# Half-token stages at the end of a two-block transformer kernel, DVE's share of the weight split, and rounded sums for three norms

## The reference

```
h = h + 0.5 * swiglu(rms(h, ffn1_norm), ffn1_w_in, ffn1_w_out)    # U_F1I, U_F1O
h = h + hybrid_mixer(rms(h, mix_norm), ...)                       # linear attention, sparse attention
h = h + 0.5 * swiglu(rms(h, ffn2_norm), ffn2_w_in, ffn2_w_out)    # U_F2I, U_F2O
h = h + sigmoid(rms(h, ple_norm) @ ple_w_gate) * (p @ ple_w_proj) # U_PLEG; U_PLEP makes the product with p
return rms(h, final_norm)

def rms(x, g):  return x * rsqrt(mean(x * x) + eps) * g
def swiglu(x, w_in, w_out):  gate, up = split(x @ w_in); return (silu(gate) * up) @ w_out
```

## Time and profile before

| | |
|---|---|
| median of 3 runs | 2160.92 us |
| profiled execution | 2160.85 us, its span 2159.0 us |
| PE busy | 2145.0 us (99% of the span) |
| DVE, ACT, POOL busy | 985.5, 756.4, 977.7 us |
| granted TensorE clock, mean of the span | 0.998 of full speed |
| chain that ended last | PE 89%, DVE 4%, POOL 2%, issue 2%, ACT 1% |
| stores of the result | 8 issues on SP, 256 KB each, landing 2.8 us after issue (median) |

### The profile page before, as it was taken

How to read it: one execution, slowest core, us unless ns; L and a number is a source line. 1 busy time by engine, 2 the same in 40 slices (tenths; PEclk the granted TensorE clock), 3 DMA queues, 4 the chain that set the end, 5 groups by cost and what they waited for, 6 DMA issues and landing times.

```text
span 2159.0 us, 31378 instructions
## 1 busy us (share of the span) xinstructions
PE 2145.0 (99%) x12524; PEld 1849.6 (86%) x12524; DVE 985.5 (46%) x1471; ACT 756.4 (35%) x1020; POOL 977.7 (45%) x777
## 2 busy tenths in 40 slices
PE   9999999999999999999999999999999999999998
PEld 8897999999999887888888788888788888888886
DVE  5244454289888208322200719651975442222026
ACT  4133455342222216322212415551346332222134
POOL 3322223466555548555544541054422555555444
PEclk9999999999999999999999999999999999999999
DMA  4321111212222223222222321123220222222222
GB/s 166 103 79 60 60 60 59 98 67 92 96 97 97 107 97 111 104 97 97 97 97 97 103 101 62 40 79 137 78 79 21 98 98 97 97 97 97 97 103 92
DMA packets 31950, 195.18 MB, mean 90 GB/s; under 512 B 3968, under 2 KB 4480, under 8 KB 10096
## 3 DMA queue, kind: packets, MB, share of 16 engines
q1 hardware_dynamic: 26784, 182.86, 23.6%
q10 hardware_dynamic: 5072, 11.00, 1.6%
HBM read 189.48 MB, written 4.23 MB: 90 GB/s over the span
## 4 chain that ended last, share of the span: by engine, by line
PE 89%; DVE 4%; POOL 2%; issue 2%; ACT 1%; DMA 0%; SPq 0%; DVEq 0%; ACTq 0%; POOLq 0%
PE ps L2456 75%; POOL wlo L726 2%; PE ps L3104 2%; PE ps L2523 2%; DVE sqa L1578 1%; PE ps L3319 1%; PE ps L3303 1%; PE ps L3239 1%; PE ps L3186 1%; DVE x2lo L1566 1%; PE ps L2771 1%; PE ps L2698 0%; DMA raw<-wstream 0%; PE ps L2733 0%; PE ps L2794 0%
## 5 line engine op out<-in xcount | busy, mean ns | idle before, releaser
L726 POOL TENSOR_TENSOR wlo<-raw,whi 128x512 fp32r<-128x512 f32 (+2 forms) x768 | 973.9, 1301 | 1146.1 <-ACT whi L802 1093.8
L802 ACT CAST whi<-raw 128x2048 fp32r<-128x2048 f32 x161 | 307.7, 1911 | 814.7 <-PE ps L2456 758.4
L2456 PE MATMUL ps<-x2hi,whi 128*128 128x512 f32 x1136 | 449.0, 395 | 1.1 <-DVE x2lo L1566 1.1
L2456 PE MATMUL ps<-x2hi,wlo 128*128 128x512 f32 x1136 | 442.4, 389 | 0.0
L2456 PE MATMUL ps<-x2lo,whi 128*128 128x512 f32 x1136 | 442.1, 389 | 0.0
L2456 PE MATMUL ps<-xhi,whi 128*128 128x256 f32 (+2 forms) x1304 | 263.2, 283 | 0.9 <-DVE xlo L1566 0.5
L2456 PE MATMUL ps<-xlo,whi 128*128 128x256 f32 (+2 forms) x1304 | 260.8, 281 | 0.0
L2456 PE MATMUL ps<-xhi,wlo 128*128 128x256 f32 (+2 forms) x1304 | 260.7, 281 | 0.0
L2456 PEld LDWEIGHTS ps<-x2hi,whi 128*128 128x128 f32 x1136 | 213.3, 188 | 49.0 <-issue 5.0
L2456 PEld LDWEIGHTS ps<-x2lo,whi 128*128 128x128 f32 x1136 | 213.4, 188 | 44.7 <-issue 1.9
L2456 PEld LDWEIGHTS ps<-x2hi,wlo 128*128 128x128 f32 x1136 | 213.2, 188 | 44.8
(11 more groups left out here) (497 smaller groups left out, 2802.4 us busy)
## 6 DMA issues: line engine op xcount, KB each, us to landing
raw<-wstream SPq DMA_DIRECT2D x170, 1024.0 KB, 4.8
ncb<-c_rows ACTq DMA_DIRECT2D x8, 256.0 KB, 3.7
ple_rows<-ple_out ACTq DMA_DIRECT2D x4, 512.0 KB, 3.9
bias<-bias_rows ACTq DMA_DIRECT2D x8, 256.0 KB, 4.7
ple<-ple_rows ACTq DMA_DIRECT2D x4, 512.0 KB, 5.3
out_dram<-outb SPq DMA_DIRECT2D x8, 256.0 KB, 2.8
h_all<-h SPq DMA_DIRECT2D x1, 792.0 KB, 10.4
h_all<-h SPq DMA_DIRECT2D x2, 264.0 KB, 7.0
```

Of the source, the lines that this page charges most:

```text
L726: return nc.gpsimd.tensor_tensor(wlo[b][:, cols], raw[b][:, cols], whi[b][:, cols].bitcast(F32), ALU.subtract)
L802: nc.scalar.copy(whi[b][:], raw[b][:]).then_inc(sig("hi_done"), 1)
L2456: ins = mm(dst, w[slot][:, cols], xx(tok), start=first and p_ == 0, stop=last and p_ == 2, skip_group_check=True)
```

## The change

It has four parts.

1. *The start of U_F1I.* POOL makes only three quarters of the low weights of the first two units. DVE makes the other five inside `add_normed`, one after each of chunks 4 to 7 and one at the end. TensorE's order takes k = 0 and 1 of both units first. U_F1I+2 is rounded by quarters.
2. *Norms 4, 6 and 7* (both feed-forwards of the second block, and PLE). ACT copies the sum of squares rounded to fp32r, DVE subtracts this from the sum, and TensorE multiplies both parts by fp32r ones. The sum moves 12 matmuls later, into the unit that follows (for norm 7 behind 24 instead of 12 matmuls of U_PLEG+1). For all folded norms the refinement writes `fold` itself, without the copy.
3. *The heads' sums* come together behind the whole of U_MG1+1.
4. *The end* goes by halves of the tokens. U_PLEG+2 is scaled by two instructions. The last unit does both chunks for tokens 0 to 255, then chunk 0 and chunk 1 for tokens 256 to 511, each in its own place in PSUM. Sums, root and scaling follow for each half; the root is one power on POOL instead of ACT's and DVE's steps. Blocks 0 and 1 are scaled and stored first.

The diff, cut to its core:

```
-        PIECE = {u: P for u in (U_UP, U_UP + 1, U_PLEP, U_F1I, U_F1I + 1, U_GR + 2, U_GR + 3, U_MG1, U_DSAO + 1)}
+        PIECE = {u: P for u in (U_UP, U_UP + 1, U_PLEP, U_GR + 2, U_GR + 3, U_MG1, U_DSAO + 1)}
+        FIRST_LOW = [(U_F1I, 0), (U_F1I, 1), (U_F1I + 1, 0)]
+        LATER_LOW = {4: (U_F1I, 2), 5: (U_F1I, 3), 6: (U_F1I + 1, 1), 7: (U_F1I + 1, 2), 8: (U_F1I + 1, 3)}
...
+            for part in range(2):                                       # POOL
+                pool.wait_ge(sig("mean_out"), part + 1)
+                cols = slice(2 * part, 2 * part + 2)
+                nc.gpsimd.tensor_tensor(out_root[:, cols], out_mean[:, cols], half_col.to_broadcast([P, 2]), ALU.pow
+                                        ).then_inc(sig("root_out"), 1)
...
+            def sum_high(n):                                            # ACT
+                act.wait_ge(sig("sq_added"), adds_before(n + 1))
+                nc.scalar.copy(sum_split[:, 0, :], squares_of(n)[:, 0, :]).then_inc(sig("norm_half"), 1)
...
+                if n in SPLIT:                                          # DVE, end of folded_sums
+                    dve.wait_ge(sig("norm_half"), 2 * SPLIT.index(n) + 3)
+                    vec.tensor_tensor(sum_split[:, 1, :], squared[:, 0, :], sum_split[:, 0, :].bitcast(F32),
+                                      ALU.subtract).then_inc(sig("norm_half"), 1)
...
+                if n in SPLIT:                                          # TensorE, norm
+                    for x in range(2):
+                        ins = mm(total, one_r.to_broadcast([P, P]), sum_split[:, x, :], start=(x == 0), stop=(x == 1))
...
-                norm()
                 units_of_pair(1, False)
...
-            after_ple = [(0, 0), (0, 1), (0, 2), (1, 0), (1, 1), (0, 3), (0, 4), (1, 2), (0, 5), (1, 3), (0, 6), (0, 7)]
-            after_ple += [(1, k) for k in range(4, KC)]
+            after_ple = [(0, 0), (0, 1), (1, 0), (1, 1), (0, 2), (0, 3), (0, 4), (0, 5), (1, 2), (1, 3)]
+            after_ple += [(0, 6), (0, 7), (1, 4), (1, 5), (1, 6), (1, 7)]
...
+            mg1_tiles(1, 0, UT)
             for hd in range(4):
-                mg1_tiles(1, 4 * hd, 4 * hd + 4)
                 pe.wait_ge(sig("gn_vec"), 3 * hd + 1)
                 mm(bank(4 + hd), one_col.to_broadcast([P, P]), head_squares(hd)[0][:, 0:SEQ], start=True, stop=True
                    ).then_inc(sig("gn_used"), 1)
...
+                places = [last_banks[0][:, 0:HALF], last_banks[0][:, HALF:SEQ], last_banks[1][:, 0:HALF],
+                          last_banks[2][:, 0:HALF]]
+                for n, dst in enumerate(places):                        # TensorE, last unit
+                    tokens, c = (EARLY, LATE)[n // 2], n % 2
...
+            sums(0, sq_sum, 0, True)                                    # TensorE, behind the last unit
+            sums(0, sq[0], 0)
+            sums(0, sq[0], HALF, last=True).then_inc(sig("total_done"), 1)
+            turn(0, 0)
+            turn(1, 0)
+            turn(0, 1)
+            turn(1, 1)
+            sums(1, sq_sum, HALF, True)
+            sums(1, sq[1], 0)
+            sums(1, sq[1], HALF, last=True).then_inc(sig("total_done"), 1)
+            turn(2, 0)
+            turn(3, 0)
+            turn(2, 1)
+            turn(3, 1)
```

More of the change, by code:

```diff
@@ L1488, in _ @@
                 scale_out(2 * i + 1)
[L1489 to L1503, removed]
+            gate(2, slice(4, 5))
@@ L2416, in sum_up @@
                                       ).then_inc(sig("sq_added"), 1)
-            for i in range(3):
+            for i in range(2):
                 u = U_PLEG + i
@@ L2480, in unit @@
                         low_ready(quarters, k // 2)
-                    if sums is not None and (c, k) == (0, 4):
+                    if sums is not None and (c, k) == divmod(sums_at, KC):
                         sums()
@@ L3043, in units_of_pair @@
                         pe.wait_ge(sig("gate_ready"), i + done)
-                    unit(b, SEQ, x2hi, x2lo, quarters=first)
+                    unit(b, SEQ, x2hi, x2lo, quarters=first, sums=None if after else norm)
                     pe.wait_ge(sig("lo_done"), i * 2 + (unit0 + 2))
@@ L3358, in _ @@
                     pe.wait_ge(sig("lo_done"), u + 1)
-                    unit(u % 2, SEQ, x2hi, x2lo, sums=norm if u == U_PLEG + 1 else None)
+                    unit(u % 2, SEQ, x2hi, x2lo, sums=norm if u == U_PLEG + 1 else None, sums_at=KC)
                     continue
-                for c in range(2):
+                places = [last_banks[0][:, 0:HALF], last_banks[0][:, HALF:SEQ], last_banks[1][:, 0:HALF],
+                          last_banks[2][:, 0:HALF]]
+                for n, dst in enumerate(places):
+                    tokens, c = (EARLY, LATE)[n // 2], n % 2
+                    if n == 3:
+                        pe.wait_ge(sig("pg_ready"), 4)
@@ L3372, in turn @@
+                    if n:
+                        ins.then_inc(sig("ple_done" if n < 3 else "unit_done"), 1)
+            def turn(j, half):
+                for k in range(4 * half, 4 * half + 4):
                     ins = nc.tensor.transpose(out_banks(j)[:, k * P:(k + 1) * P], fin[:, k, j * P:(j + 1) * P],
                                               ident[:])
-                    if k % 4 == 3:
-                        ins.then_inc(sig("out_turned"), 1)
-            def sums(src, first):
-                for j in range(4):
-                    ins = mm(bank(1)[:, j:j + 1], src[:, j * P:(j + 1) * P], one_col, start=(first and j == 0),
-                             stop=(not first and j == 3), skip_group_check=True)
-                return ins
@@ L3396, in _, with sums @@
-            pe.wait_ge(sig("fin_ready"), KC)
-            for j in range(3):
-                turn(j, 7, 8)
-            pe.wait_ge(sig("out_scale"), 1)
-            turn(3, 4, 8)
+                ins.then_inc(sig("out_turned"), 1)
+            def sums(part, src, first_token, first=False, last=False):
+                for j in range(2):
+                    cols = slice(first_token + j * P, first_token + (j + 1) * P)
+                    ins = mm(out_sums[part][:, j:j + 1], src[:, cols], one_col, start=first and j == 0,
+                             stop=last and j == 1, skip_group_check=True)
+                return ins
```

216 lines of the change are left out of this document (168 added, 48 removed).

## The result

The changed kernel takes 2165.32 us (median of 13 runs, 2165.08 to 2166.82) against 2160.92 for the kernel before (13 runs): a ratio of 1.0021, with a 95% interval from 1.0014 to 1.0028. The interval lies above 1, so the kernel is slower, by about the 0.2% that the prediction called no change. The span grew by 5.1 us, from 2159.0 to 2164.1; the profiled execution, at 2165.94 us, lies 0.6 above the median, so the traces show a little more loss than the times.

The account below looks back on a forecast made before the run. TensorE bounds the kernel, busy 2145.0 of 2159.0 us. Against 2160.85 us profiled, -1.8 - 0.4 + 6.2 - 2.6 = +1.4 gives 2162.25, as median 2162.3; own range 2160.8 to 2163.8, 8 in 10 from 2157.3 to 2165.7.

Parts of the forecast that it names:

- Heads' sums: Four sums behind U_MG1+1: TensorE waits for ACT's squares, weight quarters and POOL's low part; +6.2 us, bounds +5.0 to +6.5.
- by the row the sum stays +6.2: Heads' gap: the clock fell only at the trace's end, so no clock cost is added to the +6.2 us.
- rival 1: Heads' gap: the granted clock falls there; +1.5 to +3.9 us, 2163.8 to 2166.2, set at 2165.5; chance 0.25.
- First feed-forward: U_F1I, second block: waits for x's low part shrink and the sum gets cheaper; -1.8 us, bounds -2.6 to -0.4.
- depending on how much of ACT's queue moves forward: U_F1I, low part for (0,5): wanted at 841.4, ready at 842.2 to 842.5; a wait of 0.8 us taken.
- Second feed-forward: U_F2I: an fp32 sum of 0.86 us becomes two matmuls, 0.45 us; -0.4 us.
- The end: Last norm and stores by halves: only four stores left behind the second root; -2.6 us, bounds -0.3 to -3.3.
- The wait before U_PLEG+2: Last norm: first scaled evacuation done at 2123.0, TensorE wants its bank at 2122.5; a new wait of 0.5 us.
- 2: Heads' gap: it doesn't reach TensorE, as U_MG1+2's low weights come early enough; 2156.1 to 2157.1 us; chance 0.13.
- 3: Kernel's end: it gains nothing, the second half's chain being as long as the old one; 2164.9 us; chance 0.10.

Follow-up runs that it names:

- the quarter ahead of the norm: Changed kernel with heads' sums back between quarters and ACT's roundings behind chunks of x, plus DVE's third low quarter of U_F1I moved ahead of the norm: 2156.40 us.

## Why the prediction was off by 3.0 us

- **Heads' sums: the wait right, the clock left out.** With the clock kept up (24 further matmuls) the stage is 6.25 us longer than before, the predicted +6.2; POOL's end, forecast for 1424.2 and 0.6 earlier by the gain ahead of it, came at 1423.46. What failed is the sentence "by the row the sum stays +6.2": the stage lost 8.7, and 2.4 of it is the clock. I took the late fall at the end of the trace, 6 us after the last wide matmul, as a ground against rival 1. But there TensorE did transposes and sums until 2150.25, and in the gap it had little: the prediction itself counts two sums, 1.7 of 8 us. The 2.4 lie inside the +1.5 to +3.9 of rival 1, which had a chance of 0.25. In part that is luck: the 1.5 was read from slow matmuls at the kernel's start, where the same rows have the granted clock at 1.00.
- **First feed-forward: the place right, the term too large.** Forecast -1.8, measured -0.85, inside the bounds. The wait that was set at 0.8 us for (0,5), the lower end of the prediction's own 0.8 to 1.1, is 1.57 over (0,4) and (0,5), and another 0.17 comes with the sum. The step that failed is "depending on how much of ACT's queue moves forward", left unpriced: nothing moved (DVE's third low part starts at 835.02, forecast 834.59), so the new order gained nothing, and all of the -0.85 is the later sum's. The version with the new order on ACT shows that this step is worth 1.1 us.
- **Second feed-forward: right**, -0.4 forecast, -0.5 measured from U_MIXO to the last down matmul.
- **The end: right.** Forecast -2.6, measured +0.83 - 3.25 = -2.4, and -2.5 with the part alone. The wait before U_PLEG+2 is 0.4 (0.5 forecast), the second scalings start 5.5 us behind the wide work (5.5 forecast), and the span ends 10.7 behind it (11.1). The wide work itself ends 0.5 later than forecast; most of it is 0.2 around the rounded sum and 0.2 more than counted for the last unit's first low quarter.
- **The rivals.** 2 fell with the 5.5 us of waits in front of the last two sums, 3 with the end's gain. Rival 1 is what happened.
- **The sum.** In the profiled execution the heads are 2.5 above the forecast, the first feed-forward 0.95, the end 0.2, and 0.2 is there at the first mark, less 0.1 in the second feed-forward and ahead of it: 3.7 in all, from 2162.25 to 2165.94. The median lies 0.6 below that execution; in which stage is open. A smaller part of the clock in most executions would fit, but isn't shown.

## What to carry to other kernels

Before moving sums or other small work behind a unit, follow every buffer that they free: here one ACT queue held squares that waited for TensorE and weights that TensorE waited for, and more places together with another order on ACT made the move free, while another order alone gave back 4.6 us. A gap on TensorE of some microseconds with little in it is priced as the gap plus what the lower clock costs behind it (2.4 us in the changed kernel, about 1.5 with the heads' sums alone). When an edit lets TensorE run ahead of an elementwise chain, look for the next thing that TensorE takes from that chain: the order of the first feed-forward gained nothing, with or without the later sum, until ACT's order was changed too and DVE got its input earlier. A combined gain, here -0.85, says nothing of the parts until each has run alone.

## What the runs showed of the hardware

- A fall of the clock in the middle of a kernel: down near 1421.4, while TensorE stood still, and up near 1428.1, in the midst of wide matmuls. In the run with the heads' sums alone it fell and rose at the same times, near 1421.4 and 1428.2, though its sums start 1.85 us later. One started every 0.427 us in between, where 0.227 is usual.
- DVE and POOL slow each other, some instructions far more than others: DVE's addition from 0.69 to 1.75 us (changed kernel), its low quarter from 0.69 to 1.81 and POOL's pair of quarters from 2.54 to 2.98 (the quarter ahead of the norm).
- The same code starts U_PLEP at 819.2 us in the kernel before and at 820.5 in the run with the heads' sums alone, far ahead of its edit. For parts worth under one microsecond, distances inside one trace tell more than times.
